# A one-core attention and mixture-of-experts block: rounding, copying and scores in another order

## The chip, the cores and the metric

The kernel runs on one core of a Trainium2 chip. The metric is the device time of one execution in microseconds (us). The core's engines run their own instruction streams in order and meet only at semaphores: TensorE (PE), ScalarE (ACT), VectorE (DVE), GpSimd (POOL) and SyncE (SP), which issues the DMAs.

## What is computed

The reference is one transformer block on 512 tokens of width 2048, in float32: a normalisation, one large input projection, three kinds of attention, an output projection, and a mixture of 64 experts in 8 groups.

```python
h = rms_norm(x, ln1[l])
proj = h @ w_in[l]
(a_q, a_k, a_v, b_q, b_k, b_v, b_f, c_q, c_kc, c_vc, c_ks, c_vs, c_kw, c_vw,
 c_g) = jnp.split(proj, split_points, axis=-1)
...
o_a = diff_attention(...)        # two softmaxes, one minus lambda times the other
o_b = forgetting_attention(...)  # a softmax with a decay summed over positions
o_c = nsa_attention(...)         # compressed, selected and window branches, gated
mix = jnp.concatenate([o_a, o_b, o_c], axis=-1)
x = x + mix @ w_out[l]
x = x + hier_moe(rms_norm(x, ln2[l]), ...)
return rms_norm(x, ln_f)
```

The change touches only how the attention part's work is ordered. Nothing of what is computed changes.

## The kernel before

The projection is cut into 45 column tiles of 128 columns (COLUMNS). Each is 16 groups of three matmuls (L916), because every float32 weight is split in two: ScalarE rounds the tile to w_high (L1392, round_tile), GpSimd subtracts that from the tile to give w_low (L804, split_tile; from tile 34 on VectorE does it in quarters, L1903, split_quarters). Three ring buffers hold the loaded tiles and two hold w_high, so tile n + 2 can be rounded when tile n is projected.

Attention is a list of 96 steps (ALL). Twelve units follow each other: 4 diff heads with 4 steps each, 4 pairs of fox heads with 4 steps, and 4 nsa groups with 16 steps (kinds cmp, both, slc, win). Step n scores one block of 128 queries against its keys, and passes through the engines in a pipeline:

- PE: scores(n), three steps ahead (LOOK = 3), into one of two PSUM buffers. They wait for exps(n - 2).
- VectorE: row_max(n), two steps ahead, adds the bias and takes the maximum; ScalarE: exps(n), two steps ahead; VectorE: normalise(n), one step ahead.
- PE: transpose_probs(n); ScalarE and VectorE: copy_pT(n), a half each; PE: values(n), one step behind; ScalarE: out_copy(n - 1).

Between these, PE projects the tiles of the next unit in portions. The table FILL says which k range of which tile lies in half 0 (ahead of values and transposes) and half 1 (behind the transposes) of a step. For a diff or fox unit it is, taking tiles 11 to 13: 11 (v) in step 1, both halves; the turn (transposes) of 11 in step 2, half 0; 12 (q) in step 2, half 1, and step 3, half 0; 13 (k) in step 3, half 1, and step 4, half 0. Steps 5, 9, 13, 17 and 21 begin the same pattern. Step 0 has tile 8 (v) in half 0, and its turn, tile 9 and tile 10 in half 1. Steps 25 to 28 carry five tiles: 29 (v) whole in step 25, half 0, and its turn in half 1; 30 in both halves of step 26; 31 whole in step 27, half 0; 32 (k) in step 27, half 1, and step 28, half 0. Tile 33 (v) fills steps 29 to 31 and is turned in step 32. In nsa units each step has only a half 0: the k tile ends in steps 43, 59 and 75, the v tile ends in 47 and 63 and is turned in 48 and 64. From step 80 on, half 0 holds an output product (fill_out), whose sum VectorE adds (add_part).

All projections go to one PSUM bank, PJ, so each waits until the one before it has been copied out: staged_a counts ScalarE's copies (take_out at L1436, L1443 and L1445; take_turned at L1453), staged_v VectorE's copy of the k tile (L1778, L1780).

The order of the work is written out by hand, one program for each engine. ScalarE's step n is:

```python
after_fill(n, 0)       # take_out(tile), round_after(tile), take_turned(tile)
if n >= 1:
    out_copy(n - 1)
copy_pT(n)
exps(n + 2)
after_fill(n, 1)
```

VectorE's step n is after_fill(n, 0) (the copy of a k tile that ended), add_part(n), split_quarters(n, 0), row_max(n + 2), copy_pT(n), normalise(n + 1), after_fill(n, 1), split_quarters(n, 1).

Of the kernel before, what the change touches and what calls it, by code (L numbers as in the profile page):

```python
# [86 lines left out]
LOOK = 3  # L87
# [48 lines left out]
def fillings():  # L136

    out = [([], []) for _ in range(len(ALL))]
    for g in range(len(HEADS) - 1):
        lo, hi = max(START[g] - LOOK, 0), START[g + 1] - LOOK
        slots = [(n, half) for n in range(lo, hi) for half in range(2 if len(STEPS[HEADS[g][0]]) == NT else 1)]
        if len(slots) < 4:
            (n, half), last = slots[0], slots[-1]
            for i in range(FIRST[g + 1], FIRST[g + 2]):
                out[n][half].append((i, 0, KT, False))
                n, half = last
                if COLUMNS[i][1] == "v":  # L150
                    out[n][half].append((i, KT, KT, True))
            continue
        slots = slots[:-1]
        tiles = range(FIRST[g + 1], FIRST[g + 2])
        turns = sum(COLUMNS[i][1] == "v" for i in tiles)
        places, at = len(slots) - turns, 0
        for j, i in enumerate(tiles):
            parts = (j + 1) * places // len(tiles) - j * places // len(tiles)
            assert parts > 0
            for a in range(parts):  # L160
                n, half = slots[at]
                out[n][half].append((i, a * KT // parts, (a + 1) * KT // parts, False))
                at += 1
            if COLUMNS[i][1] == "v":
                n, half = slots[at]
                out[n][half].append((i, KT, KT, True))
                at += 1
        assert at == len(slots)
    return out


FILL = fillings()


def filling(n, half):
    return FILL[n][half]
# [149 lines left out]
def hybrid_block_moe_kernel(nc, x_in, ln1, w_in, diff_lambda, diff_subln, fox_bf, cmp_pos_k, cmp_w1_k,  # L326
# [3 lines left out]
    with ExitStack() as ctx:  # L330
# [539 lines left out]
        def _(pe):  # L870
# [215 lines left out]
                ins = out_products(PJ[:], ALL_TILES + m, t, True, True)  # L1086
                ins.then_inc(part_ready, 1)

            for n in range(LOOK):
                scores(n)  # L1090
            for n in range(ALL_STEPS):
                fill(n, 0)
                fill_out(n)
                if n >= 1:
                    values(n - 1)
                transpose_probs(n)
                fill(n, 1)
                if n + LOOK < ALL_STEPS:
                    scores(n + LOOK)
# [277 lines left out]
        def _(act):  # L1377
# [16 lines left out]
            def round_after(n):  # L1394
                if n + 2 < ALL_WEIGHTS:
                    round_tile(n + 2)
# [124 lines left out]
            def copy_pT(n):  # L1521
# [2 lines left out]
                w = P if kind == "cmp" else (qb + 1) * P * (2 if kind == "both" else 1)  # L1524
                fn(cmp_pT if kind == "cmp" else pT[:, 0, 0:w], PT[:, 0, 0:w], ACT.Copy).then_inc(pT_copied_a, 1)

            def after_fill(n, half):
                for tile, lo, hi, turns in filling(n, half):
                    if lo < hi == KT:
                        take_out(tile)  # L1530
                        round_after(tile)
                    if turns:
                        take_turned(tile)

            def out_copy(n):
                g, kind, u, pr, qb = ALL[n]
# [18 lines left out]
            for n in range(ALL_STEPS):  # L1555
                after_fill(n, 0)
                if n >= 1:
                    out_copy(n - 1)
                copy_pT(n)
                if n + 2 < ALL_STEPS:  # L1560
                    exps(n + 2)
                after_fill(n, 1)
                if out_group(n) is not None and out_group(n)[1] == NT - 1:
                    round_after(ALL_TILES + out_group(n)[0])
                if n == NSA0:
                    root(dss, NT + 1)
                if n == START[-2] - LOOK:
                    act.wait_ge(projected, ALL_TILES)
                    round_mix(1)
                if n == START[-2] + 7:  # L1570
                    round_mix(2)
# [124 lines left out]
        def _(dve):  # L1696
# [237 lines left out]
            row_max(1)  # L1934
            normalise(0)
            for n in range(ALL_STEPS):
                after_fill(n, 0)
                add_part(n)
                split_quarters(n, 0)
                if n + 2 < ALL_STEPS:  # L1940
                    row_max(n + 2)
                copy_pT(n)
                if n + 1 < ALL_STEPS:
                    normalise(n + 1)
                after_fill(n, 1)
                split_quarters(n, 1)
                if n == FOX0 + 2:
                    dve.wait_ge(out_done, OUTS[FOX0])
                if n in range(FOX0 + 2, NSA0, 4):
                    diff_squares((n - FOX0) // 4)  # L1950
                if n == NSA0 - 1:
                    v.tensor_scalar(dss, dss, 1.0 / (2 * HD), EPS, ALU.mult, ALU.add).then_inc(ms_ready, 1)
                if n == NSA0 + 1:
                    dve.wait_ge(root_ready, NT + 1)
                    link(v.reciprocal(drs, dss))
                if n in range(NSA0 + 2, NSA0 + 2 + NT):
                    diff_scale(n - NSA0 - 2)
                if n == NSA0 + 2 + NT:
                    dve.sem_inc(diff_ready, 1)
# [265 lines left out]
```

## Time and profile before

| | us |
|---|---|
| median of 3 runs | 2003.47 (2003.39 to 2005.43) |
| span of the profiled execution | 2002.0 |
| PE busy | 1888.2, 94% |
| VectorE busy | 693.8, 35% |
| ScalarE busy | 561.2, 28% |
| GpSimd busy | 287.7, 14% |

The first 137 us are the normalisation and the first tiles, the attention steps last until about 853 us, and the output projection and the experts take the rest. How to read it: PE is the engine that is nearly always busy, and a share of busy time of the others says little. What counts is where PE is idle, for whom, and what that engine did just before. PEclk is the granted TensorE clock as a share of 2.4 GHz: 1.00 and 0.50 are its two levels here.

### The profile page before, as it was taken

The numbers are of one execution on the slowest core, as the hardware profiler recorded it, in microseconds if no ns is written. First come the engines' busy times: TensorE is split into PE (matmuls) and PEld (weight loads), VectorE is DVE, ScalarE is ACT, GpSimd is POOL, SyncE is SP. The second block draws the span as 40 slices with busy tenths as digits, with TensorE's granted clock in tenths as the row PEclk, the third lists the DMA queues.
The fourth block names the chain that finished last, engine by engine and source line by source line (L and its number), as shares of the span: only waits on it lengthen the run. The fifth ranks groups of instructions, "written<-read, shape, count | busy, mean of one in ns | idle before, by whom it ended". The sixth has DMA issues, their size and how long they took to land.

```text
span 2002.0 us, 28095 instructions
## 1 busy us (share of the span) xinstructions
PE 1888.2 (94%) x11846; PEld 1341.4 (67%) x11846; DVE 693.8 (35%) x1639; ACT 561.2 (28%) x1163; POOL 287.7 (14%) x240
## 2 busy tenths in 40 slices
PE   6999999999999998999999999999998999999997
PEld 5887777777777676788875666555555655556554
DVE  4331222543856658711151222213222222222222
ACT  5322232323444444432321221212112121211211
POOL 2433433433000003355200000000000000000000
PEclk9999999999999999999999999999999999999999
DMA  9452322324222213145469999999999999999994
GB/s 288 124 161 75 79 79 69 84 64 95 43 58 59 53 44 126 43 140 187 147 282 415 429 417 427 426 428 428 426 426 427 420 422 420 422 424 410 427 427 184
DMA packets 175661, 505.88 MB, mean 253 GB/s; under 512 B 52642, under 2 KB 135970, under 8 KB 148906
## 3 DMA queue, kind: packets, MB, share of 16 engines
q1 hardware_dynamic: 173226, 495.63, 64.7%
q0 software_dynamic: 2304, 8.39, 1.0%
q8 instruction: 96, 1.57, 0.3%
q14 instruction: 35, 0.29, 0.0%
HBM read 495.85 MB, written 16.53 MB: 256 GB/s over the span
## 4 chain that ended last, share of the span: by engine, by line
PE 91%; issue 3%; DVE 3%; ACT 2%; DMA 1%; POOL 0%; SPq 0%; POOLq 0%; ACTq 0%; DVEq 0%
PE banks L916 25%; PE banks L1310 19%; PE banks L1340 12%; PE banks L1070 9%; PE banks L1283 6%; PE banks L1311 3%; PE banks L1230 3%; PE banks L1022 2%; PE banks L1003 2%; PE banks L1050 2%; PE banks L1231 1%; PE banks L965 1%; PE banks L1150 1%; PE banks L1010 1%; PE banks L1324 0%
## 5 line engine op out<-in xcount | busy, mean ns | idle before, releaser
L916 PE MATMUL banks<-ht_rounded,ring_rounded 128*128 128x512 f32 x1056 | 361.2, 396 | 4.9 <-ACT at_region L1453 4.9
L916 PEld LDWEIGHTS banks<-ht_rounded,ring_rounded 128*128 128x128 f32 x1056 | 196.8, 189 | 58.9 <-issue 14.2
L1311 PE MATMUL banks<-at_region,ht_region 128*64 128x256 f32 x896 | 200.1, 382 | 0.0
L1310 PE MATMUL banks<-at_region,ht_region 128*64 128x256 f32 x864 | 192.9, 382 | 6.0 <-issue 6.0
L804 POOL TENSOR_TENSOR ring_rounded<-ring_region,ring_rounded 128x512 fp32r<-128x512 f32 x100 | 127.2, 1304 | 469.9 <-ACT ring_rounded L1392 469.9
L2126 DVE TENSOR_TENSOR ring_region<-ring_region,banks 64x256 f32<-64x256 f32 x64 | 27.1, 423 | 381.3 <-ACT ring_region L1644 381.2
L1310 PEld LDWEIGHTS banks<-at_region,ht_region 128*64 128x64 f32 x864 | 118.5, 138 | 58.6 <-issue 19.1
L804 POOL TENSOR_TENSOR ring_rounded<-ring_region,at_rounded 128x512 fp32r<-128x512 f32 (+1 forms) x100 | 126.6, 1298 | 203.9 <-ACT at_rounded L1392 203.9
L1644 ACT ACTIVATE ring_region<-banks 64x256 f32<-64x256 f32 x64 | 24.2, 378 | 457.1 <-PE banks L1311 457.1
L916 PE MATMUL banks<-ht_rounded,at_rounded 128*128 128x512 f32 x352 | 143.9, 409 | 5.6 <-ACT at_region L1453 4.9
L1310 PE MATMUL banks<-x_region,ht_region 128*64 128x256 f32 x608 | 136.2, 383 | 2.6 <-issue 2.6
L916 PE MATMUL banks<-mix_rounded,at_rounded 128*128 128x512 f32 x352 | 138.4, 393 | 0.0
L916 PE MATMUL banks<-mix_rounded,ring_rounded 128*128 128x512 f32 x352 | 138.0, 392 | 0.0
L1311 PE MATMUL banks<-x_region,ht_region 128*64 128x256 f32 x576 | 130.8, 386 | 0.0
L1070 PE MATMUL banks<-ring_rounded,ht_rounded 128*128 128x512 f32 x384 | 129.8, 392 | 0.8 <-POOL x_rounded L811 0.8
L843 POOL DMA_INDIRECT out<-mix_region,g_idx x8 | 8.1, 1007 | 844.3 <-DVE mix_region L2146 844.3
L1283 PE MATMUL banks<-ring_region,consts 64*128 64x512 f32 x512 | 127.2, 615 | 0.0
L1311 PEld LDWEIGHTS banks<-at_region,ht_region 128*64 128x64 f32 x896 | 122.8, 138 | 0.0
L2135 DVE COPY ring_region<-banks 128x512 f32<-128x512 f32 x64 | 44.2, 691 | 213.7 <-PE banks L1340 213.7
L1340 PE MATMUL banks<-at_region,consts 128*64 128x512 f32 x448 | 104.0, 605 | 13.0 <-issue 10.3
L1310 PEld LDWEIGHTS banks<-x_region,ht_region 128*64 128x64 f32 x608 | 83.7, 138 | 39.3 <-issue 12.0
L1650 ACT ACTIVATE ring_region<-banks 128x512 f32<-128x512 f32 x64 | 38.2, 597 | 253.8 <-PE banks L1340 253.8
(290 smaller groups left out, 3390.5 us busy)
## 6 DMA issues: line engine op xcount, KB each, us to landing
at_region<-in_w_gate SPq DMA_DIRECT2D x27, 2048.0 KB, 21.1
at_region<-in_w_up SPq DMA_DIRECT2D x27, 2048.0 KB, 19.9
at_region<-in_w_down SPq DMA_DIRECT2D x27, 2048.0 KB, 23.2
x_region<-in_w_gate SPq DMA_DIRECT2D x19, 2048.0 KB, 21.8
ring_region<-in_w_in SPq DMA_DIRECT2D x36, 1024.0 KB, 6.0
x_region<-in_w_up SPq DMA_DIRECT2D x18, 2048.0 KB, 18.9
x_region<-in_w_down SPq DMA_DIRECT2D x17, 2048.0 KB, 25.2
ring_region<-in_w_down SPq DMA_DIRECT2D x10, 2048.0 KB, 23.2
```

The source lines that it names most:

```text
L804: ins = nc.gpsimd.tensor_tensor(w_low[n % RING][:, ks, 0:width], ring[n % RING][:, ks, 0:width], w_high[n % 2][:, ks, 0:width].bitcast(F32 ...
L916: ins = mm(out, w[:, k, 0:width], h[:, k, :], start=k == 0 and i == 0, stop=k == KT - 1 and i == 2)
L1003: ins = mm(S[:, par, half, 0:W], q[pr][rows, cols], keys[kind == "win"][rows, 0:W], start=True, stop=True)
L1022: ins = nc.tensor.transpose(PT[:, half, kb * P:(kb + 1) * P], probs[:, n % 2, half, kb * P:(kb + 1) * P], ident)
L1050: ins = mm(o, v[:, kb, cols], pT[:, half, j * P:(j + 1) * P], start=kind == "fox" and kb == 0, stop=part != "slc" and kb == qb)
L1070: ins = mm(out, a[:, 4 * c + i, t * P:(t + 1) * P], b[:, i, :], start=first and i == 0 and k == 0, stop=last and i == 3 and k == 2)
L1230: mm(place[turn[j]][:, 0:HALF], hi[:, j, :], slots, start=True, stop=False)
L1283: ins = mm(acc[:, 2 * side + m, :], spread[e8 % 2][rows, :], y_sb[rows, m, :], start=e8 == 0, stop=e8 == PER - 1)
L1310: mm(PJ[0:CAP, 0:D_EXPERT], x, gate[j], start=j == 0, stop=j == KT - 1)
L1311: ins = mm(PJ[CAP:2 * CAP, 0:D_EXPERT], x, up[j], start=j == 0, stop=j == KT - 1)
L1340: ins = mm(PT[side * CAP:(side + 1) * CAP, m, :], hidT[:, j, :], down[:, j, (2 * side + m) * T:(2 * side + m + 1) * T], start=j == 0, stop ...
L2135: v.tensor_copy(y_sb[:, 1, :], PT[:, 1, :]).then_inc(y_v, 1)
```

## The change

Three orders are changed; no instruction is added or taken away.

1. PE: the first three scores were issued ahead of step 0. Now scores(0) and scores(1) are, then the projection of tile 8 (fill(0, 0)), then scores(2).
2. ScalarE: a tile that has been projected is put on a list, and the rounding of the tile two further on is done by round_finished, called behind exps(n + 2) and again behind after_fill(n, 1), the second time only if that tile begins at (n + 1, 0) or earlier (BEGINS).
3. VectorE: row_max(n + 2) comes first in the step, ahead of add_part and split_quarters. Where a k tile ends in half 0, normalise(n + 1) and then the copy of k come ahead of copy_pT(n).

```diff
+BEGINS = {tile: (n, half) for n in range(len(ALL)) for half in range(2) for tile, lo, hi, _ in FILL[n][half] if lo == 0}
...
-            for n in range(LOOK):
+            for n in range(LOOK - 1):
                 scores(n)
+            fill(0, 0)
+            scores(LOOK - 1)
             for n in range(ALL_STEPS):
-                fill(n, 0)
+                if n > 0:
+                    fill(n, 0)
                 fill_out(n)
...
+            finished = []
+
             def after_fill(n, half):
                 for tile, lo, hi, turns in filling(n, half):
                     if lo < hi == KT:
                         take_out(tile)
-                        round_after(tile)
+                        finished.append(tile)
                     if turns:
                         take_turned(tile)
+
+            def round_finished(before=None):
+
+                while finished and (before is None or BEGINS.get(finished[0] + 2, before) <= before):
+                    round_after(finished.pop(0))
...
                 if n + 2 < ALL_STEPS:
                     exps(n + 2)
+                round_finished()
                 after_fill(n, 1)
+                round_finished(before=(n + 1, 0))
...
             for n in range(ALL_STEPS):
-                after_fill(n, 0)
+                ends_k = any(COLUMNS[tile][1] == "k" and lo < hi == KT for tile, lo, hi, _ in filling(n, 0))
+                if n + 2 < ALL_STEPS:
+                    row_max(n + 2)
                 add_part(n)
                 split_quarters(n, 0)
-                if n + 2 < ALL_STEPS:
-                    row_max(n + 2)
+                if ends_k:
+                    normalise(n + 1)
+                    after_fill(n, 0)
                 copy_pT(n)
-                if n + 1 < ALL_STEPS:
+                if not ends_k and n + 1 < ALL_STEPS:
                     normalise(n + 1)
```

## Rows read from the trace of the kernel before

**Rows 1.** The page, part 1: busy time of each engine.

```profile
PE 1888.2 (94%) x11846; PEld 1341.4 (67%) x11846; DVE 693.8 (35%) x1639; ACT 561.2 (28%) x1163; POOL 287.7 (14%) x240
```

**Rows 2.** PE's waits, 195 to 860 us: sum in us, times, longest.

```profile
PE banks L1022 <- DVE at_region L1887: 7.6, 4, 2.2
...
PE banks L916 <- ACT at_region L1453: 6.8, 7, 2.9
...
PE banks L1022 <- DVE at_region L1877: 0.9, 1, 0.9
```

**Rows 3.** Windows of 1 us: PE busy (instructions), granted clock, DMA share, GB/s.

```profile
142.00:143.00 1.00, 1.00 (x5) 0.50 0.00 0
...
456.00:457.00 1.00, 1.00 (x5) 1.00 1.28 206
...
667.00:668.00 1.00, 1.00 (x4) 0.50 0.00 0
...
755.00:756.00 1.00, 1.00 (x4) 0.50 1.11 467
```

**Rows 4.** Timeline, step 0: start, duration, engine, line; idle time in brackets.

```profile
138.34 4.93 POOL L804 TENSOR_TENSOR ring_rounded<-ring_region,ring_rounded 128x512 fp32r<-128x512 f32 x4 [9.04 <-ACT ring_rounded L1392]
...
141.09 1.65 PE L1003 MATMUL banks<-at_region 64*128 64x384 f32 x4 [2.55 <-ACT at_region L1517]
...
143.34 0.41 DVE L1845 TENSOR_REDUCE small<-banks 128x2 f32<-128x256 f32 x1
...
156.51 1.90 ACT L1392 ACTIVATE at_rounded<-ring_region 128x2048 fp32r<-128x2048 f32 x1
...
158.46 0.58 ACT L1517 ACTIVATE at_region<-banks,small 128x384 f32<-128x384 f32 x1
...
159.58 0.61 ACT L1453 ACTIVATE at_region<-banks 128x512 f32<-128x512 f32 x1
...
160.24 0.73 PE L916 MATMUL banks<-ht_rounded,ring_rounded 128*128 128x512 f32 x2 [2.92 <-ACT at_region L1453]
```

**Rows 5.** Chain of waits, in order of time: one tile's 48 matmuls.

```profile
469.13 11.17 PE banks L916 x48
```

**Rows 6.** Timeline, steps 26 and 27, tile 32's rounding and split first.

```profile
468.98 1.91 ACT L1392 ACTIVATE at_rounded<-ring_region 128x2048 fp32r<-128x2048 f32 x1
...
470.96 5.04 POOL L804 TENSOR_TENSOR ring_rounded<-ring_region,at_rounded 128x512 fp32r<-128x512 f32 x4 [12.40 <-ACT at_rounded L1392]
...
481.04 1.09 PE L1022 MATMUL banks<-consts,at_region 128*128 128x128 f32 x8
...
483.27 0.48 ACT L1517 ACTIVATE at_region<-banks,small 128x256 f32<-128x256 f32 x1
```

**Rows 7.** Timeline, steps 1 and 2.

```profile
193.64 0.21 ACT L1517 ACTIVATION_READ_ACCUMULATOR at_region<-banks,small 128x1 f32 x1
...
199.18 0.49 PE L1022 MATMUL banks<-consts,at_region 128*128 128x128 f32 x3
...
200.53 0.50 PE L916 MATMUL banks<-ht_rounded,at_rounded 128*128 128x512 f32 x1 [0.86 <-ACT at_region L1453]
```

**Rows 8.** Timeline, step 26, PE.

```profile
455.82 0.50 PE L916 MATMUL banks<-ht_rounded,at_rounded 128*128 128x512 f32 x1 [2.94 <-ACT at_region L1453]
```

**Rows 9.** Timeline, steps 47 and 48.

```profile
600.44 0.59 ACT L1525 ACTIVATE at_region<-banks 128x512 f32<-128x512 f32 x1
...
602.29 0.62 ACT L1453 ACTIVATE at_region<-banks 128x512 f32<-128x512 f32 x1
...
602.82 0.64 PE L999 MATMUL banks<-kcT,at_region 64*128 64x32 f32 x8
```

**Rows 10.** Timeline, steps 43 and 44.

```profile
574.55 1.40 DVE L1778 COPY at_region<-banks 64x512 f32<-64x512 f32 x2 [1.87 <-PE banks L916]
...
575.98 0.69 DVE L1845 TENSOR_REDUCE small<-banks 128x2 f32<-128x512 f32 x1
...
578.87 1.06 PE L1022 MATMUL banks<-consts,at_region 128*128 128x128 f32 x8 [2.23 <-DVE at_region L1887]
```

## The prediction

> **What bounds the kernel now.** I read the page first: TensorE (PE) is busy for 94% of the span [rows 1], so an edit of ScalarE's and VectorE's order can gain only what PE idles for in the 96 attention steps (about 137 to 853 us), plus what the slow clock costs behind an idle stretch. Then the table of waits shows for whom PE idles there [rows 2]: 7.6 us in four waits for VectorE's normalising (L1887), 6.8 us in seven waits for ScalarE's copy of the turned values (L1453), and little else. Last the timeline, to see which instruction of the waiting engine came too late, and the granted clock in windows of 1 us [rows 3]. The output projection and the experts behind 853 us are untouched, and there PE goes on in its own order.
>
> **Part 1, the third scores behind the projection.** Now PE stops behind scores(1): scores(2) starts at 141.09 after 2.55 us idle for the first exponentials [rows 4]. Behind that idle the granted clock is at its lower level (0.50, which is 1.2 of 2.4 GHz) [rows 3]; scores(2) take 1.65 us, and the windows of the clock stand at half from 141 to 147 (one of the six is shown), so some 2.8 us of work are lost too: 0.7 in the scores and 2.1 in the projection behind them. In the new order tile 8's projection (48 matmuls, 11.2 us at full clock [rows 5]) starts at 138.54 and ends at 149.7. Nothing that it needs is late: GpSimd had been idle for 9.0 us when it began tile 9's split at 138.34 [rows 4], so tile 8's was done by 129.3. The price comes next. exps(2), which ScalarE's copy of turned tile 8 follows, now needs scores(2) (0.9 us), row_max(2) (from the 0.41 us reduction at 143.34 to the end 1.4 us [rows 4]), the exponentials (158.46 to 159.7, 1.2 us) and tile 10's rounding (1.9 us), which moves from ahead of them to behind them but still ahead of the turned copy (0.6 us): 149.7 + 0.9 + 1.4 + 1.3 + 1.8 + 0.6 = 155.7. PE has scores, transposes and turn done at 151.5 and idles 4.3 us, where it now idles 2.92 (and 0.58 before the turn). Tile 9 then starts at 155.8, not at 160.24. If the clock falls there as it did behind the 2.92 us (tile 9 took 12.8 us from 160.24 to 173.05 instead of 11.2, cost 1.6), the whole lead of **4.4 us** stays. Bounds: the clock doesn't fall, 6.0; it falls for as long as in 141 to 147, 3.2.
>
> **Part 2, rounding behind exponentials, four kinds of place.** The rounding is 1.9 us, GpSimd's split behind it 5.0 us [rows 6].
> (a) Steps 2, 6, 10, 14, 18, 22: the v tile is turned, and its copy (L1453) waits behind the rounding [rows 7]: PE ends its transposes at 199.67 and starts the next projection at 200.53. With the rounding deferred the copy starts as soon as the turn is done (198.9), ending 0.1 ahead of PE's need. Five of the six gaps go: 0.85 + 0.86 + 0.86 + 0.23 + 0.23 = **3.0 us** (6.8 less step 2's 0.86 and step 25's 2.94). In step 2 another wait takes its place: tile 12 is now rounded behind exps(3), which ended at 193.85 [rows 7], so it is split at 193.8 + 1.9 + 5.0 + 0.1 = 200.8, where PE wants it at 199.7: 1.1 instead of 0.86, **-0.3**. In later heads the tile at the same place is rounded two steps earlier relative to its need and has some 6 us of slack.
> (b) Step 25 [rows 8]: projection and turn lie in one step, so the deferred rounding still stands ahead of the turned copy, and now starts only behind exps(27), which wait for the transposes. ScalarE ends 0.35 later: **-0.35**.
> (c) Steps 26 and 27, the dear one. Tile 30 ends in half 1 of step 26. Tile 32 begins in half 1 of step 27, and round_finished(before=(27, 0)) lets through only what begins at (27, 0) or earlier. So tile 32, now rounded at 468.98 and split by 476.0 [rows 6], is rounded behind exps(29) in step 27, and those wait for the transposes of that step, which end at 482.13 [rows 6]. ScalarE: copy of pT 0.6 us, exponentials 1.0 us (from the row of one at 483.27, a pair), rounding 1.9 us: 485.5. GpSimd: 5.0 us, 490.6. PE, which now goes straight on at 482.1, waits **8.5 us**. Tile 33 follows it on ScalarE and GpSimd (done some 5 us later), in time for step 29. Behind an idle this long I add 1.6 us for the lower clock: **-10.1**. Bounds: 0 (after 2.94 us idle in step 25 the clock stayed at 1.00 [rows 3]) and 2.8 for the clock.
> (d) Steps 32, 48, 64: the last v tile of a head ends one step earlier, and its rounding now starts behind the exponentials, right ahead of the turned copy in the next step. Today the rounding runs while ScalarE would wait for PE's transposes anyway; then copy at 600.44, exponentials, turned copy at 602.29, done before PE ends scores at 603.46 [rows 9]. New: copy 600.4 to 601.0, exponentials to 602.4, rounding to 604.2, turned copy to 604.8: PE waits 1.35 us. In step 32 the same sum gives 1.05. Together **-3.75**. Bounds: none of it can be hidden unless ScalarE's work ran beside itself; a fall of the clock (some 1.9 us, below) could join each. Queued behind the turned copy are the next copies and exps(n + 2); behind VectorE's wait for the later rounding (its first quarter of a split) stand row_max and normalise of the next steps. I follow step 43 to 45: normalise(45) ends at 583.5, PE needs it at 583.9, so it just fits.
>
> **Part 3, VectorE: maxima first, k's copy behind normalising.** In steps 44, 60 and 76 PE waits 2.23 us for normalise(n), because VectorE stood waiting for the end of the k projection, copied k (1.40 us from 574.55) and only then took row_max (from 575.98) and the normalising [rows 10]. In the new order row_max(45) and normalise(44) run from 572.7 to 575.5, during the projection, and k's copy ends at 576.9, before PE's next projection at 578.8 wants the bank. PE's transposes follow at 576.64: **2.2 us** each. In two of the three places the clock fell after the gap (0.50 at 667 to 668 and at 755 to 756 [rows 3], nearly four windows each, half of which is 1.9 us): step 60 gives 2.2 + 1.9 = **4.1**. In step 76 it also fell, but ScalarE's late rounding of tile 46 (752.0 to 753.9) holds its copy of pT back and opens a new wait of 1.0, and the mix's rounding and split behind it are still the chain: I follow them to PE's first output product, from 769.0 to 766.3, **2.7**. The bound below for each is 0 with another wait in its place, the bound above 4.1.
> In the steps with output products row_max runs while PE multiplies, and the addition follows at once; of the 0.94 us wait for L1877 [rows 2] I count **0.7**; between 0 and 0.9. Elsewhere k's copy (0.69 us) starts when its projection ends, as now: nothing, since the two operations ahead of it are ready during the projection.
>
> **Sum.** 4.4 + 3.0 - 0.3 - 0.35 - 10.1 - 3.75 + 2.2 + 4.1 + 2.7 + 0.7 = 2.6 us less on PE. The profiled execution has a span of 2002.0 us; the median of the runs is 2003.47, 1.5 us above. I put the 2.5 on the median: **2001.0 us**, no change that this kernel's measurement (about 0.2%, 4 us) can tell.
>
> **Rivals.** (1) The clock stays high behind both long waits, as it did behind 2.94 us in step 25: 2 x 1.6 = 3.2 less, 1997.8. For: that row; against: it fell behind 2.55, behind 2.92 and in two of three waits of 2.23. Chance 0.22.
> (2) Slower, one mechanism: the turned copies of (d) come behind a rounding in three steps, and each idle lets the clock fall as it did behind the wait of 2.23 us that ended at 665. Price 3 x 1.9 = 5.7 and 1.2 more behind the first wait: 2007.9. It decides when all three fall; two give 2006. Against: waits of 0.8 to 0.9 at 763 to 769 left the clock at 1.00. Chance 0.13. The Trainium skill ("TensorE: Matmul & The Clock Gate", section "What's actually happening") says the clock is granted by how busy the array has been lately and not by single instructions. By that rule short waits in a thinly filled stretch could tip it; the sum would be this rival's. The rows agree in part, since equal waits of 2.23 us gave both levels.
> (3) VectorE's queue: in the first three nsa heads it waits for w_rounded at the first quarter of a split, with row_max and normalise of the next step behind it. My slack for step 45 is 0.4 us, and the gains of part 3 in steps 44 and 60 would be given back (2.2 + 2.2 of them): 2005.4. Chance 0.15.
> (4) Tile 32 is not late, because I misread when its rounding is let through: 10.1 less, 1991. The diff is plain on it: 0.05.
> The forecast's own case has 0.45, 1999.3 to 2003.2.
>
> **How the numbers follow.** Faster by over 0.2% (under 1999.5): rivals 1 and 4 and a sliver of my own case, 0.30. Slower (over 2007.5): part of rival 2 and joined mishaps, 0.11. Same: 0.59. The range from 1996.5 to 2007.0 leaves out rival 4, the far part of rival 2 and the ends of the others.
>
> **What would show it.** Tile 32: ScalarE's rounding near 480 instead of 467 us, PE idle about 8.5 us ahead of the second half of step 27, released by GpSimd L804. Part 1: no PE wait between scores(1) and tile 8, and a wait of about 4.3 us for L1453. (a): the 0.86 us gaps gone; (d): three new waits of 1.0 to 1.4 for L1453. Part 3: L1022's waits for L1887 gone in steps 44, 60, 76. I am wrong if PE's idle time in step 27 is under 5 us, if the k reordering opens a wait for VectorE's copies of pT, or if the clock spends more than some 12 us at half in the attention steps.

## The result, and the profile after

| | before | after |
|---|---|---|
| median of 19 runs each, us | 2003.67 (1999.37 to 2006.77) | 2006.88 (2004.86 to 2008.32) |
| ratio, with its 95% interval | | 1.0014 (1.0008 to 1.002) |
| span of the profiled execution, us | 2002.0 | 2004.1 |
| mean granted clock over all timed runs | 0.9897 (51 runs of three further jobs) | 0.9888 (19 runs) |

By the ratio the change costs 2.8 us, with an interval of 1.6 to 4.0; the medians lie 3.2 us apart. The forecast was 2.5 us the other way. The time lies in the range (1996.5 to 2007.0) and within the 0.2% that was to count as no change, but the sign is wrong, and 19 runs of each are enough to see it. So the question is where 5 us went. The granted clock gives a first hint, and a weak one: its mean is 0.0009 lower, which is 1.8 us of 2004, but the three jobs' own means for the kernel before already lie between 0.9894 and 0.9901. A 52nd run of the kernel before, in the first of these jobs, took 8017.81 us and is left out of this mean and of every ratio.

First part 1 of the page of the kernel after, which answers to [rows 1]. The columns are busy time, share of the span, number of instructions:

```profile
PE 1885.2 (94%) x11846; PEld 1339.6 (67%) x11846; DVE 678.7 (34%) x1639; ACT 564.7 (28%) x1163; POOL 285.1 (14%) x240
```

The counts are the same and the busy times differ by little. As before, one has to look at PE's waits. These are the largest of them in the attention steps of the kernel after (137 to 860 us; sum in us, times, longest), and the one that is left for the normalising, to be held against [rows 2]:

```profile
PE banks L919 <- ACT at_region L1459: 11.5, 5, 4.4
PE banks L919 <- POOL ring_rounded L807: 9.9, 2, 8.5
PE banks L1046 <- ACT at_region L1531: 2.0, 2, 1.2
...
PE banks L1025 <- DVE at_region L1902: 0.9, 1, 0.9
```

Line numbers have moved a little: PE's by 3 (L916 is L919, L1022 is L1025), ScalarE's turned copy from L1453 to L1459 and its rounding from L1392 to L1398, VectorE's normalising from L1887 to L1902, GpSimd's split from L804 to L807. Three things are seen. The normalising (L1902) has gone from 7.6 us in four waits to 0.9 in one. A wait for GpSimd's split (L807) that was not there has 9.9 us in two places. The waits for the turned copy have gone from seven in [rows 2] (eight with step 0's) to five, but these are longer.

The timeline of the kernel after shows each at its place (start, duration, engine, line; idle time in brackets). Step 0, step 2, step 25:

```profile
151.56 1.90 ACT L1398 ACTIVATE at_rounded<-ring_region 128x2048 fp32r<-128x2048 f32 x1
153.36 0.59 ACT L1459 ACTIVATE at_region<-banks 128x512 f32<-128x512 f32 x1
154.00 1.22 PE L919 MATMUL banks<-ht_rounded,ring_rounded 128*128 128x512 f32 x2 [4.37 <-ACT at_region L1459]
...
195.55 0.47 PE L919 MATMUL banks<-ht_rounded,at_rounded 128*128 128x512 f32 x1 [1.37 <-POOL ring_rounded L807]
...
447.27 0.79 PE L919 MATMUL banks<-ht_rounded,at_rounded 128*128 128x512 f32 x1 [3.24 <-ACT at_region L1459]
```

Step 27, tile 32, and then step 32, the first of three such places (the others, at 610.83 and 696.72, are 1.28 long as well):

```profile
477.12 0.47 ACT L1523 ACTIVATE at_region<-banks,small 128x256 f32<-128x256 f32 x1
...
477.57 1.91 ACT L1398 ACTIVATE at_rounded<-ring_region 128x2048 fp32r<-128x2048 f32 x1
...
479.56 4.93 POOL L807 TENSOR_TENSOR ring_rounded<-ring_region,at_rounded 128x512 fp32r<-128x512 f32 x4 [27.78 <-ACT at_rounded L1398]
484.64 0.77 PE L919 MATMUL banks<-ht_rounded,at_rounded 128*128 128x512 f32 x1 [8.50 <-POOL ring_rounded L807]
...
520.90 1.93 ACT L1398 ACTIVATE ring_rounded<-ring_region 128x2048 fp32r<-128x2048 f32 x1
522.71 0.61 ACT L1459 ACTIVATE at_region<-banks 128x512 f32<-128x512 f32 x1
523.37 0.50 PE L919 MATMUL banks<-ht_rounded,at_rounded 128*128 128x512 f32 x1 [1.28 <-ACT at_region L1459]
```

In both stretches the order in time is what the prediction says: exponentials, rounding, and only then the split or the turned copy that PE stands waiting for. GpSimd had been idle for 27.78 us when it could begin tile 32's split. In step 32 the turned copy starts as the rounding ends, and PE's next projection starts when the copy ends.

Idle lengths are half of the account; the other half is the granted clock. The columns of the windows are: window, us, PE busy (instructions), PE's weight loads, VectorE, ScalarE, GpSimd, granted clock, DMA share, GB/s. The kernel after, behind the waits of steps 27 and 32:

```profile
486.00:487.00 1.00, 1.00 (x4) 0.75 (x3) 0.00 (x0) 0.00 (x0) 1.00 (x2) 0.50 0.00 0
526.00:527.00 1.00, 1.00 (x4) 0.71 (x4) 0.94 (x3) 0.98 (x3) 0.00 (x0) 0.50 0.00 0
```

Both stand at 0.50, which is 1.2 of 2.4 GHz. The prediction's sum reckoned with the first and not with the second.

### The profile page after: what moved, and what is told of

Its sections match the earlier page's. It is cut to its first block, busy times and chain, and to the rows that moved or that the text cites. A ratio compares the mean times of both kernels' runs of the same rounds, so it can differ in the third digit from the quotient of the medians.

```text
span 2004.1 us, 28096 instructions
## 1 busy us (share of the span) xinstructions
PE 1885.2 (94%) x11846; PEld 1339.6 (67%) x11846; DVE 678.7 (34%) x1639; ACT 564.7 (28%) x1163; POOL 285.1 (14%) x240
## 4 chain that ended last, share of the span: by engine, by line
PE 91%; issue 3%; ACT 2%; DVE 2%; POOL 1%; DMA 1%; SPq 0%; POOLq 0%; ACTq 0%; DVEq 0%
PE banks L919 25%; PE banks L1316 19%; PE banks L1346 12%; PE banks L1073 9%; PE banks L1289 6%; PE banks L1317 3%; PE banks L1025 3%; PE banks L1236 3%; PE banks L1006 2%; PE banks L1053 2%; PE banks L1237 1%; PE banks L968 1%; PE banks L1156 1%; PE banks L1013 1%; POOL ring_rounded L807 1%
## 5 line engine op out<-in xcount | busy, mean ns | idle before, releaser
L919 PE MATMUL banks<-ht_rounded,ring_rounded 128*128 128x512 f32 x1056 | 363.4, 398 | 4.4 <-ACT at_region L1459 4.4
L919 PEld LDWEIGHTS banks<-ht_rounded,ring_rounded 128*128 128x128 f32 x1056 | 198.1, 191 | 57.8 <-issue 13.5
L807 POOL TENSOR_TENSOR ring_rounded<-ring_region,ring_rounded 128x512 fp32r<-128x512 f32 x100 | 126.7, 1298 | 458.4 <-ACT ring_rounded L1398 458.4
L919 PE MATMUL banks<-ht_rounded,at_rounded 128*128 128x512 f32 x352 | 145.6, 414 | 17.6 <-POOL ring_rounded L807 9.9
L807 POOL TENSOR_TENSOR ring_rounded<-ring_region,at_rounded 128x512 fp32r<-128x512 f32 (+1 forms) x100 | 124.6, 1277 | 224.2 <-ACT at_rounded L1398 224.2
L919 PE MATMUL banks<-mix_rounded,at_rounded 128*128 128x512 f32 x352 | 140.2, 398 | 0.0
L919 PE MATMUL banks<-mix_rounded,ring_rounded 128*128 128x512 f32 x352 | 138.3, 393 | 0.0
L1316 PE MATMUL banks<-x_region,ht_region 128*64 128x256 f32 x608 | 134.5, 379 | 2.9 <-issue 2.8
L1317 PE MATMUL banks<-x_region,ht_region 128*64 128x256 f32 x576 | 127.5, 379 | 0.0
```

Source lines behind the costliest of these rows:

```text
L807: ins = nc.gpsimd.tensor_tensor(w_low[n % RING][:, ks, 0:width], ring[n % RING][:, ks, 0:width], w_high[n % 2][:, ks, 0:width].bitcast(F32 ...
L919: ins = mm(out, w[:, k, 0:width], h[:, k, :], start=k == 0 and i == 0, stop=k == KT - 1 and i == 2)
L1316: mm(PJ[0:CAP, 0:D_EXPERT], x, gate[j], start=j == 0, stop=j == KT - 1)
L1317: ins = mm(PJ[CAP:2 * CAP, 0:D_EXPERT], x, up[j], start=j == 0, stop=j == KT - 1)
```

## The experiments

All times are compared with runs of the kernel before in the same job: medians 2003.92 (first job: both plain repeats, parts 1 and 3 alone), 2005.04 (part 2 alone, tile 32, filled wait, four mends) and 2004.62 (nsa value tiles, both second repeats).

### The two kernels again

No edit. One profile is one draw of the clock, so both kernels were profiled again, twice.

> The kernel before, unchanged, one more profiled execution. Theory (the clock's fall behind an idle stretch is decided anew in each execution): PE's idle stretches stand at the same places with the same lengths (2.55 and 2.92 us in step 0, 2.94 us at step 26, 2.23 us in steps 44, 60, 76), but the windows at half clock behind them differ from the first profile's in at least one place (there it fell in step 0 twice, in steps 60 and 76, and not at 26 and 44). Rival (each place has its own fixed outcome): the same four places as before, the same windows.

> The changed kernel, unchanged, one more profiled execution. Theory (falls are decided anew in each execution): idle of 4.4 us in step 0, 3.2 us at step 26, 8.5 us in step 27 and 1.3 us in steps 32, 48, 64 as in its first profile; the clock falls surely behind 8.5 and 4.4 us, and differs from the first profile at 3.2 us or at one of the 1.3 us stretches. Rival (fixed by place): falls at 154, 446, 481 and 524 us again, none elsewhere.

> The kernel before, unchanged, a third profiled execution. Theory (idle fixed, falls of the clock anew each time): idle lengths as in the two others within 0.03 us, half clock behind another set of the same idles; the end of the attention steps within 3 us of 853. Rival (only attention differs between executions): the time from the end of attention to the end of the span is the same within 0.5 us as in the other two (it was 1151.2 and 1153.8 us from the last step's transposes, which speaks against it).

> The changed kernel, unchanged, a third profiled execution. Theory: idle lengths as in its two others, the clock falls behind 8.5, 4.4 and the first 1.28 us again (three of three), and may or may not behind 3.2 us at step 26 and behind 1.28 us at step 65. Rival (something behind the attention steps is slower in the changed kernel): from the last step's transposes to the end over 1154 us.

Measured: before 2007.25 and 2005.04 (spans 2005.5 and 2003.2), after 2006.63 and 2007.63 (spans 2004.8 and 2005.8). The idle lengths came back to within 0.03 us. The clock did not, as the expectations had it. This is step 25 in the second profile of before, its PE row of the timeline and its window, to be held against [rows 8] and the second row of [rows 3]:

```profile
455.69 0.80 PE L916 MATMUL banks<-ht_rounded,at_rounded 128*128 128x512 f32 x1 [2.94 <-ACT at_region L1453]
```

```profile
456.00:457.00 1.00, 1.00 (x3) 0.81 (x3) 0.00 (x0) 0.00 (x0) 1.00 (x1) 0.50 1.25 200
```

The same kernel, the same 2.94 us of idle time, the same work behind it, and 0.50 in place of 1.00; the third profile had 1.00 again. In the first profile of the kernel after and in its second repeat, step 25's wait of 3.24 was followed by 0.50, in its first repeat by 1.00. The table below shows the price. It gives the time from one step's transposes to a later step's, read off the timelines, for each profile in the order of taking (from, to):

| stretch | before | after |
|---|---|---|
| first scores to step 1 | 54.08, 54.16, 54.06 | 50.16, 49.88, 50.06 |
| 25 to 26 | 10.72, **13.29**, 10.72 | **13.56**, 11.05, **13.44** |
| 26 to 28 | 33.01, 33.02, 33.02 | 44.41, 43.79, 44.34 |
| 32 to 33 | 3.82, 3.82, 3.82 | 6.62, 6.63, 6.62 |
| 48 to 49 | 3.69, 3.69, 3.69 | 5.04, 5.06, 5.06 |
| 64 to 65 | 3.68, 3.69, 3.69 | 5.04, **6.58**, 5.04 |
| 43 to 45 | 10.55, 10.55, 10.55 | 8.58, 8.58, 8.58 |
| 59 to 61 | **12.12**, 10.59, **12.15** | 8.59, 8.57, 8.58 |
| 75 to 77 | 8.71, 8.72, 8.70 | 6.08, 6.08, 6.08 |
| first scores to last transposes | 713.15, 714.26, 713.13 | 716.57, 714.68, 716.28 |

Where the clock doesn't fall, a stretch repeats to 0.05 us. Where it falls in some executions, the bold ones, the price is 2.4 to 2.6 us in step 25 and 1.5 in steps 60 and 64. Where it falls in all of them, a stretch can still move: by 0.3 us up to step 1 and by 0.6 from 26 to 28 in the kernel after, because the fall comes at another moment. So the mean of the last row rose by 2.3 us (713.5 to 715.8), which lies in the timed interval of 1.6 to 4.0.

### Part 1 alone

```diff
-            for n in range(LOOK):
+            for n in range(LOOK - 1):
                 scores(n)
+            fill(0, 0)
+            scores(LOOK - 1)
             for n in range(ALL_STEPS):
-                fill(n, 0)
+                if n > 0:
+                    fill(n, 0)
```

> Part 1 alone: the kernel before with scores(2) behind the projection of tile 8; ScalarE and VectorE as before. Theory: scores(2) no longer stops PE for 2.55 us, and the half clock behind it goes. ScalarE rounds tile 10 right behind its copy of tile 8, while PE and VectorE make scores(2) and their maxima, so the turned copy comes some 0.5 us earlier than in the changed kernel: PE idle about 3.7 instead of 4.4 us. About 6 us less, 1998 (1995 to 2000). Rival (the third scores are merely late at another place and the clock falls twice anyway): within 2 us of before.

Measured: 1999.21 (1996.36 to 2002.01), ratio 0.9973 (0.9964 to 0.9983), 5.4 us less, as the theory had it. PE's wait ahead of tile 9 was 2.72 us (3.7 expected): with the rounding still ahead of the exponentials, ScalarE is through 1.65 us sooner than in the full change (4.37). From the first scores to step 1's transposes it took 47.7, not 54.1: 6.4 less. So part 1 is worth 6.4 us by itself in that profile, and 4.1 when part 2 puts tile 10's rounding behind exps(2).

### Part 3 alone

```diff
-                after_fill(n, 0)
+                ends_k = any(COLUMNS[tile][1] == "k" and lo < hi == KT for tile, lo, hi, _ in filling(n, 0))
+                if n + 2 < ALL_STEPS:
+                    row_max(n + 2)
                 add_part(n)
                 split_quarters(n, 0)
-                if n + 2 < ALL_STEPS:
-                    row_max(n + 2)
+                if ends_k:
+                    normalise(n + 1)
+                    after_fill(n, 0)
                 copy_pT(n)
-                if n + 1 < ALL_STEPS:
+                if not ends_k and n + 1 < ALL_STEPS:
                     normalise(n + 1)
```

> Part 3 alone: VectorE's order of the changed kernel, PE and ScalarE as before. Theory: the three waits of 2.23 us for normalise in steps 44, 60, 76 and 0.7 of the 0.94 us in step 85 go, 7.4 us, and up to 4 us of half clock behind them: 7 to 11 less, 1994.5 (1992.5 to 1997). Rival (ScalarE's rounding ahead of its copies becomes the wait as soon as VectorE is early): new waits for ScalarE's copy of pT (L1525) in those three steps, gain under 4 us.

Measured: 1999.3 (1995.38 to 2001.61), ratio 0.9974 (0.9965 to 0.9983), 5.2 us less. The timeline of this kernel in steps 43 and 44, against [rows 10]:

```profile
572.93 1.00 DVE L1887 TENSOR_SCALAR at_region<-at_region,small 128x512 f32<-128x512 f32 x2
573.96 1.40 DVE L1778 COPY at_region<-banks 64x512 f32<-64x512 f32 x2
...
574.36 1.91 ACT L1392 ACTIVATE at_rounded<-ring_region 128x2048 fp32r<-128x2048 f32 x1
...
576.34 0.27 ACT L1525 ACTIVATE at_region<-banks 128x128 f32<-128x128 f32 x1
576.66 1.09 PE L1022 MATMUL banks<-consts,at_region 128*128 128x128 f32 x8 [1.42 <-ACT at_region L1525]
```

VectorE is in time now: normalise(44) is over at 573.9, and PE is ready for it at 575.2 (576.66 - 1.42). But the wait isn't gone. It is 1.42 instead of 2.23, and its releaser is ScalarE, whose copy of pT stands behind the rounding. So only 0.8 of the 2.2 us per place belongs to part 3 alone. The rest comes when part 2 takes that rounding out of the way: in the full change the stretch from step 43 to 45 is 8.58, here 10.08 (and 10.55 before: behind the 1.42 a further wait of 0.24, for the exponentials, is new). This lies between the two expectations: the rival's waits for L1525 are there in all three steps, and the gain is larger than its 4 us.

### Part 2 alone

The edit against the kernel before, with BEGINS and round_finished as in the change:

```diff
+            finished = []
...
-                        round_after(tile)
+                        finished.append(tile)
...
                     exps(n + 2)
+                round_finished()
                 after_fill(n, 1)
+                round_finished(before=(n + 1, 0))
```

> Part 2 alone: ScalarE's order of the changed kernel, PE and VectorE as before. Theory (the late rounding of tile 32 and the turned copies behind a rounding outweigh the six short waits removed): plus 8.5 us idle and 2.9 us of half clock in step 27, plus 3 x 1.3 in steps 32, 48, 64, plus 0.5 in step 2 and 0.3 at steps 0 and 26, some 2 more of clock, less 3.8 for the waits behind the turns: plus 12 to 16, about 2018. Rival (the loss comes from the three parts working on each other): slower by less than 6 us alone.

Measured: 2021.04 (2014.54 to 2025.49, four runs), ratio 1.0083 (1.0061 to 1.0105), 16.6 us more, at the far end of the theory's 12 to 16. The waits of 8.49, of 1.28 (three times) and of 2.23 (three times) are all there, and the clock fell behind more of them (step 44 as well). It fell even behind a wait of 0.88 us, in step 79 (with one of 0.85 just ahead of it, in PE's row at 780.82):

```profile
783.21 1.60 PE L1025 MATMUL banks<-consts,at_region 128*128 128x128 f32 x7 [0.88 <-DVE at_region L1899]
```

```profile
784.00:785.00 1.00, 1.00 (x7) 0.67 (x5) 0.17 (x2) 0.00 (x0) 1.00 (x2) 0.50 0.00 0
```

But behind the 2.55 us of step 0, where it had fallen in all three profiles of before, it didn't: the stretch from the first scores to step 0's transposes was 15.36 us here and 18.2 to 18.3 there. So part 2 is the one that loses. The parts add up to -5.4 - 5.2 + 16.6 = +6.0 where the whole is +2.8; with intervals of 2, 2 and 4 us to either side that difference is a weak one. Two effects of the parts on each other are seen, of opposite signs: the 1.42 us of the run above, which the full change removes at three places, and the 2.3 us (6.4 less 4.1) that part 1 loses to part 2.

### Tile 32 let through

```diff
-                round_finished(before=(n + 1, 0))
+                round_finished(before=(n + 1, 1))
```

> The changed kernel with one condition wider: round_finished(before=(n + 1, 1)), which lets through one more tile, 32. Theory: the idle of 8.5 us in step 27 goes with the 2.9 us of half clock behind it, 11.4 less than the changed kernel: 1995.5 (1993 to 1998). Rival (the clock is lost at another place instead, since it falls somewhere in any case): 8.5 less, 1998.4 or more. Second rival (ScalarE or GpSimd is late with something else behind tile 32): PE idle over 2 us elsewhere in steps 26 to 29.

Measured: 1996.11 (1990.91 to 1998.22), ratio 0.9958 (0.9944 to 0.9972). Against the full change (1.0014) that is 0.0056 x 2004 = 11.2 us less, as the theory had it (11.4). The stretch from step 26 to 28 was 33.01, as in the kernel before to 0.01. PE's waits of this kernel for the split, in the attention steps:

```profile
PE banks L919 <- POOL ring_rounded L807: 1.4, 1, 1.4
```

One of two is left, step 2's. This one limit, a half step too strict, turns a gain of 8.4 us (0.0042 x 2004) into a loss.

### The wait for tile 32 filled with matmuls

The question was whether the 2.7 us beyond the idle 8.5 come from the clock. The edit puts 35 matmuls of 512 columns, whose product is overwritten, ahead of PE's wait for tile 32's split, so that PE is busy in the same stretch:

```diff
+                    if n == 32:
+                        for _ in range(35):
+                            mm(PJ[:], hT_high[:, 0, 0:P], hT_high[:, 0, :], start=True, stop=True)
```

> The changed kernel with 35 matmuls of 512 columns, whose result is overwritten, where PE would idle for tile 32 (about 8.2 us of the 8.5). Theory: the wait's end stays where it was, but the clock stays at 1.00 behind it, and the kernel is 2.9 us faster than the changed one, 2004.0 (2002.5 to 2005.5): that is the price of the clock by itself. Rival (half clock costs little, the 11.4 us at step 27 have another cause, such as VectorE held up by GpSimd): within 1 us of the changed kernel.

Measured: 2006.0 (1997.72 to 2010.01), above the expected 2002.5 to 2005.5 (the kernel before has 2005.04 in this job, 1.4 more than at first), ratio 1.0001 (0.9987 to 1.0014). That is 2.6 us less than the change by the ratios, but the two intervals overlap, and these 12 runs scatter over 12 us where those of the change scatter over 3.5; why isn't known. The timed runs don't decide it. The profile does. The filler's row of the timeline, and the window that stood at 0.50 in the kernel after:

```profile
477.74 7.89 PE L930 MATMUL banks<-ht_rounded 128*128 128x512 f32 x34
```

```profile
486.00:487.00 1.00, 0.81 (x4) 0.68 (x5) 0.00 (x0) 0.00 (x0) 1.00 (x2) 1.00 0.00 0
```

The clock stayed at 1.00, and the stretch from step 26 to 28 took 41.81 instead of 43.79 to 44.41, 2.4 less than their mean, though PE still couldn't start tile 32 earlier. So of step 27's price 8.5 us are the wait and 2.4 to 2.7 the clock.

### The rounding behind the nsa value tiles done at once

A finished tile lets the tile two further on be rounded. Behind the value tiles 29, 33, 37 and 41 that is tile 31, 35, 39 and 43 (the expectation names only the last three).

```diff
                         take_out(tile)
-                        finished.append(tile)
+                        if COLUMNS[tile][1] == "v" and HEADS[COLUMNS[tile][0]][0] == "nsa":
+                            round_after(tile)
+                        else:
+                            finished.append(tile)
```

> The changed kernel with tiles 35, 39 and 43 rounded as soon as the v tile before is done, as in the kernel before. Theory: the three idles of 1.28 us ahead of steps 33, 49 and 65 go, 3.8 us, and with them the half clock that fell at step 33 in every profile that has this idle and at step 65 in some: 5.5 to 7 less than the changed kernel in all, a ratio to before of 0.9981 (0.9972 to 0.9990). Rival (the clock falls some steps later instead): 3.8 less, ratio 0.9995, and the three profiles' windows show the same half clock elsewhere between 500 and 760 us.

Measured: 2000.84 (1996.75 to 2004.85), ratio 0.998 (0.9971 to 0.9989): 6.8 us less than the change. PE's waits of this kernel for ScalarE's turned copy and for the split:

```profile
PE banks L919 <- POOL ring_rounded L807: 9.9, 2, 8.5
PE banks L919 <- ACT at_region L1459: 7.3, 2, 4.4
```

Five waits for L1459 have become two (steps 0 and 25), and in its profile the clock falls nowhere between 500 and 760 us, where the rival had it fall instead. The stretches behind steps 32, 48 and 64 are 3.82, 3.69 and 3.68, those of before. By the three profiles of after this takes away 2.8, 1.4 and 1.9, together 6.0, and 0.3 of step 25, where the wait was 2.94 again with tile 31 rounded at once: 6.3 against 6.8 measured.

### Four mends together

Tile 32 let through as above, and the rounding behind the nsa value tiles done at once; in addition tile 12 rounded at once behind tile 10, so that its split is in time in step 2, and the turned copies of steps 0 and 25 issued directly behind copy_pT, ahead of the exponentials and the rounding:

```diff
                         finished.append(tile)
+                        if tile == 10 or (COLUMNS[tile][1] == "v" and HEADS[COLUMNS[tile][0]][0] == "nsa"):
+                            round_finished()
-                    if turns:
+                    if turns and (n, half) not in ((0, 1), (25, 1)):
                         take_turned(tile)
...
                 copy_pT(n)
+                if n in (0, 25):
+                    take_turned(filling(n, 1)[0][0])
...
-                round_finished(before=(n + 1, 0))
+                round_finished(before=(n + 1, 1))
```

> The changed kernel with four places of ScalarE's order mended: tile 32 let through; tiles 12, 35, 39 and 43 rounded as soon as the tile before is done, as in the kernel before; the turned copies of steps 0 and 25 directly behind copy_pT, ahead of exponentials and rounding. Theory (all that is left of the loss is those waits and their clock): 11.4 less than the changed kernel for tile 32, 3.8 and 1 to 2 of clock for steps 32, 48, 64, 3.8 and 1.7 for step 0, 1.4 for step 2, 3.0 and up to 2.5 for step 26: 1979 (1976 to 1984). Rival (exponentials put behind the turned copies become late and open waits of their own): 1985 or more.

Measured: **1980.44** (1977.94 to 1982.44, four runs), ratio 0.9886 (0.9871 to 0.99). It beats both kernels, by 22.8 us and by 25.7, and lies within its expectation. PE's row of its timeline in step 0, and its waits for the turned copy:

```profile
151.02 0.73 PE L919 MATMUL banks<-ht_rounded,ring_rounded 128*128 128x512 f32 x2 [0.69 <-ACT at_region L1459]
```

```profile
PE banks L919 <- ACT at_region L1459: 2.3, 2, 1.6
```

The 4.37 us of step 0 are 0.69, the 3.24 of step 25 are 1.60, no projection waits for GpSimd's split any more, and every window of 1 us in the attention steps stands at 1.00. The stretch from step 25 to 26 is 9.38, which neither of the two kernels reaches. Of the 25.7 us the two mends that ran alone measured 11.2 and 6.8. The rest, 7.7, is that of steps 0, 2 and 25, which had no run of their own; in this one profile their stretches are 5.9, 1.4 and 3.3 us shorter than the mean of the change.

Not tried: filling the other waits with matmuls, which would have priced the clock at each place apart. Where PE waits for the turned copy, the bank PJ is still being read, so the filler above can't go there as it stands.

## Why the prediction was wrong

Its own steps, with the mean of three profiles of each kernel (the change of the stretches above, in us on PE; those that the table above doesn't show are read from the timelines in the same way):

| step of the sum | forecast | measured | idle forecast | idle measured |
|---|---|---|---|---|
| part 1 | -4.4 | -4.07 | 4.3 | 4.37 |
| (a) turned copies | -3.0 | -3.84 | 0 | 0 |
| step 2 | +0.3 | +0.48 | 1.1 | 1.37 |
| (b) step 25 | +0.35 | +1.11 | 3.3 | 3.24 |
| (c) tile 32 | +10.1 | +11.16 | 8.5 | 8.50 |
| (d) step 32 | +1.05 | +2.80 | 1.05 | 1.28 |
| (d) step 48 | +1.35 | +1.36 | 1.35 | 1.28 |
| (d) step 64 | +1.35 | +1.87 | 1.35 | 1.28 |
| part 3, step 44 | -2.2 | -1.97 | 0 | 0 |
| step 60 | -4.1 | -3.04 | 0 | 0 |
| step 76 | -2.7 | -2.63 | 1.0 | 1.16 |
| output steps | -0.7 | -0.74 | 0.2 | 0.21 |
| sum | -2.6 | +2.3 (+2.5 in these rows, -0.2 in the stretches between them) | | |

The same in two sums. From the first scores to the last transposes PE idles 25.6 us in each profile of before and 27.8 in each of after, 2.2 more; the forecast's idle lengths add up to 1.8 more. What the lower clock costs while PE is busy (1 less the granted clock, times PE's busy share, over the windows of 1 us) is 8.2, 9.3 and 8.2 us before and 9.8, 7.8 and 9.5 after: 0.5 more by the means. The forecast had 4.4 less for it (2.6 and 1.8). So nearly all of the miss is the clock.

**What held.** Every wait of the forecast is there, at its place, with its releaser, and within 0.3 us of its length. Tile 32 is the plain case: the two lines of the diff said it, and the run that let it through took the whole of it back. Rival 1 failed: the clock fell behind both long waits, step 0's and step 27's, in every profile that has them. Rivals 3 and 4 failed too. VectorE's queue behind w_rounded opened no wait (the stretches from 43 to 45 and from 59 to 61 are the shortest of all), and tile 32 was late. The wait that part 3 gives way to (rival 3's question, whether something else stands where the wait stood) did exist, though not on VectorE: with part 3 alone it is ScalarE's rounding, 1.42 us. The forecast had it right for the full change and didn't see that the gain belonged to two parts together.

**What failed: the price of the clock, step (b), (c), (d) and step 60.** Together they miss by 0.76 + 1.06 + 1.75 + 0.01 + 0.52 + 1.06 = 5.2 us, and the idle lengths explain next to nothing of it; the other rows miss by -0.1 in all (part 1 and step 2 gave less than forecast, the turned copies 0.8 more). For step 27 the run with the filled wait shows that it is the clock: the same wait, 2.4 us less. The forecast took each place's clock from one profile of before, as if it belonged to the kernel: 0 behind 2.94 us, 1.6 behind the long wait, 1.9 back in step 60. The 1.9 was itself too large: the windows behind steps 60's and 76's waits sum to 1.7 us lost in the profile it was read from, and the stretches give 1.5 and 1.0. Over all the profiles of this case (before and after three times each, the experiments once each) the clock fell:

| wait | fell | price on PE when it fell |
|---|---|---|
| 2.55 us, step 0 | 4 of 5 | 1.6 to 2.9 |
| 4.37 us, step 0 | 6 of 6 | within part 1's -4.07 |
| 8.50 us, step 27 | 5 of 5 | 2.3 to 3.0 |
| 3.24 us, step 25 | 4 of 6 | 2.4 to 2.7 |
| 2.94 us, step 25 | 2 of 6 | 2.6 to 2.7 |
| 2.23 us, steps 44, 60, 76 | 1, 4 and 4 of 5 | 1.5 (steps 44, 60), 1.0 (step 76) |
| 1.42 us, steps 44, 60, 76 (part 3 alone) | 0, 1 and 0 of 1 | 1.6 |
| 1.28 us, step 32 | 6 of 6 | 1.5 |
| 1.28 us, step 48 | 0 of 6 | |
| 1.28 us, step 64 | 3 of 6 | 1.5 |

(Step 0's price is 16.95 and 18.3 less 15.36, from the first scores to its transposes. The 1.5 is 12.12 - 10.59 and 12.13 - 10.6 in the table of stretches and in the runs of parts 1 and 2 alone; the 1.0 is 8.71 - 7.68; step 32's is 6.62 - 3.82 - 1.28.) The one profile of before that the forecast was made from shows step 25 without a fall and step 60 with one; of the three executions, one and two had them. The biggest single miss is step 32: rival 2 named this mechanism, gave it 0.13 and asked for all three places. It came true in the first place always, in the third in half of the profiles, in the second never: of its 6.9 us about 2.0 came (1.5 and 0.5). That its 2007.9 lies near the measured 2006.88 is partly (b), (c) and step 60, which it didn't speak of. The rival had argued from waits of 0.8 to 0.9 near 763 to 769 that short ones leave the clock alone; in the run of part 2 alone it fell behind such a wait, at 783. In part 1 there was luck: the forecast counted on winning back the 2.8 us of clock behind step 0's 2.55 us, which the three profiles of before all lose and the run of part 2 alone does not.

The prediction's last sign of being wrong, over some 12 us at half clock in the attention steps, came true (27.3, 23.9 and 27.3 us), but it could tell nothing: the kernel before has 17.0, 20.5 and 17.1.

**The rule on the clock.** The rows show that the length of a wait alone doesn't decide; the stretch and the execution do: behind 1.28 us of idle time the clock fell six times in six at one place and never at another, and behind 2.94 us it fell in two profiles of six with the same work around it. The Trainium skill ("TensorE: Matmul & The Clock Gate", section "What's actually happening") says that the gate follows recent activity and that the monitor runs freely, not in step with the kernel, so that a kernel meets it at another phase in every run. These profiles agree with it, in that step 25's price was 2.4 to 2.7 in some executions and 0 in others. The prediction quoted the first half of that rule and left out the second, by which one profile can't tell what a wait costs.

**What is left open.** The stretches give +2.3, the timed runs +2.8 (1.6 to 4.0), so nothing measurable is missing. Why step 32's wait always costs the clock and step 48's never isn't shown. The work outside the attention steps scatters between executions as well: the first scores begin between 136.1 and 138.4 us, and from the last transposes to the end it takes 1151.2, 1153.8 and 1151.7 us before and 1151.5, 1153.0 and 1151.9 after. So spans of single profiles differ by up to 3.5 us with no edit at all, mostly by what lies behind the attention steps; the stretches leave both out for that reason. With three profiles of each kernel the clock's part in them is itself a small sample.

## What to carry to other kernels

Where work is deferred behind something, look at both ends: whether the limit that lets it through reaches every item (here one tile, begun half a step later than the limit, slipped a whole step and cost 11.2 us of 25.7), and whether the engine was idle in the place that the work leaves (the rounding behind the nsa value tiles had run while ScalarE would have waited anyway; moved, it cost 6.8). Price a wait as its length, which one profile gives to 0.03 us, plus a chance of a clock fall, which takes several profiles of the same kernel. And put what another engine is waiting for (the turned copy) ahead of what only has to be done some time (rounding, exponentials): that order, in steps 0 and 25, is most of what the last kernel gains beyond the two mends that ran alone (9.2 of 10.6 us by its one profile).

## What the runs showed of the hardware that wasn't expected

A wait of 1.28 us was followed by half clock six times in six at one place, and a wait of 2.94 us by none in four profiles of six (the table above). Time lost to a fall came in nearly equal pieces, 1.5 us in steps 32, 44, 60 and 64 and 2.4 to 2.7 in step 25.

VectorE's normalising is much slower beside GpSimd's split. In the kernel after the two normalising operations of a step, which took 1.00 us in the run of part 3 alone (572.93, above), took 2.98 when GpSimd began its split of the mix at the same moment:

```profile
766.06 2.98 DVE L1902 TENSOR_SCALAR at_region<-at_region,small 128x512 f32<-128x512 f32 x2
...
766.09 5.31 POOL L814 TENSOR_TENSOR x_rounded<-x_region,ht_rounded 128x512 fp32r<-128x512 f32 x4 [23.78 <-ACT ht_rounded L1564]
```

It is so wherever the two meet in these kernels' attention steps: the pair takes 1.00 us where GpSimd is idle and 2.0 to 3.1 where a split runs beside both. Not every operation of VectorE is slowed: its copy of 128x512 from PSUM at 770.23, beside the same split, took the usual 0.69. The slow one sits on the path there (PE waits 0.87 us for L1902 behind it) in both kernels alike, so it plays no part in the difference.
